# All 24 half matrices of the first four experts get homes of their own, LayerNorm parameters are spread by TensorE, identity products fill TensorE's waits

## The reference

```
for l in range(DEPTH):                                   # DEPTH = 2
    mix = hybrid_mixer(x, w_in[l], w_ret_o[l], w_dsa_o[l], w_out[l])
    h = layer_norm(DEEPNORM_ALPHA * x + mix, ln1_g[l], ln1_b[l])
    ffn = hierarchical_moe(h, ...)     # each row: 2 of 32 SwiGLU experts
    x = layer_norm(DEEPNORM_ALPHA * h + ffn, ln2_g[l], ln2_b[l])

expert_block: (silu(xb @ w_gate[e]) * (xb @ w_up[e])) @ w_down[e]
```

## Time and profile before

| what | us |
|---|---|
| median of 3 runs (1638.46 to 1639.27) | 1638.96 |
| the profiled execution | 1637.93 |
| its span in the trace | 1636.1 |

### The profile page before, as it was taken

One profiled execution on the slowest core, in us unless ns is written; L12 is line 12 of the kernel. 1 busy time (PEld: TensorE's weight loads), 2 busy tenths in 40 slices (PEclk: granted clock), 3 DMA queues, 4 the chain that ended last, 5 costly groups with the idle time before them and its releaser, 6 DMA issues. The chain is left out here.

```text
span 1636.1 us, 20903 instructions
## 1 busy us (share of the span) xinstructions
PE 1278.9 (78%) x8502; PEld 864.8 (53%) x8502; DVE 621.0 (38%) x1049; ACT 379.9 (23%) x423; POOL 0.2 (0%) x4
## 2 busy tenths in 40 slices
PE   8999999998546656656699999999985566556646
PEld 7998789984212212212188987899842122112211
DVE  5788576654100100100277875865631001000102
ACT  4334634322000000000143346343220000000000
POOL 0000000000000000000000000000000000000000
PEclk9999999999878877878889999999997688778778
DMA  8455346689999999999945453374999999999996
GB/s 297 157 195 198 121 155 228 215 355 419 427 424 428 429 429 424 428 428 429 404 169 181 155 205 133 126 278 167 411 418 428 427 427 428 427 427 427 428 426 248
DMA packets 96501, 528.72 MB, mean 323 GB/s; under 512 B 5425, under 2 KB 9905, under 8 KB 66737
## 3 DMA queue, kind: packets, MB, share of 16 engines
q1 hardware_dynamic: 94560, 523.10, 79.3%
q10 hardware_dynamic: 1872, 4.66, 0.8%
HBM read 526.69 MB, written 1.05 MB: 323 GB/s over the span
## 5 line engine op out<-in xcount | busy, mean ns | idle before, releaser
L912 PE MATMUL psum<-ring,aqT 128*32 128x512 f32 x1536 | 284.5, 715 | 131.0 <-PEq L900 131.0
L1510 DVE TENSOR_TENSOR w_low<-ring,w_high 128x2048 fp32r<-128x2048 f32 (+2 forms) x108 | 239.8, 2260 | 69.1 <-DVEq L1509 67.8
L1111 ACT ACTIVATE w_high<-ring 128x2048 fp32r<-128x2048 f32 (+2 forms) x108 | 198.5, 1887 | 193.8 <-ACTq L1108 179.5
L912 PE MATMUL psum<-spare,aqT 128*32 128x512 f32 x256 | 136.5, 724 | 116.9 <-PEq L963 116.9
L912 PEld LDWEIGHTS psum<-ring,aqT 128*32 128x32 f32 x1536 | 73.3, 129 | 234.9 <-issue 234.9
L1728 DVE TENSOR_TENSOR qk<-psum,qk 128x512 f32<-128x512 f32 x16 | 11.1, 692 | 488.1 <-DVEq L1727 488.1
L912 PE MATMUL psum<-rv,tmp 128*32 128x512 f32 x240 | 122.8, 702 | 66.0 <-PEq L988 66.0
L662 PE MATMUL psum<-x_high,w_high 128*128 128x256 f32 x512 | 146.8, 287 | 0.0
L662 PE MATMUL psum<-x_high,w_low 128*128 128x256 f32 x512 | 143.3, 280 | 0.0
L662 PE MATMUL psum<-x_low,w_high 128*128 128x256 f32 x512 | 143.2, 280 | 0.0
L912 PEld LDWEIGHTS psum<-spare,aqT 128*32 128x32 f32 x256 | 30.3, 130 | 211.0 <-issue 211.0
(11 more groups left out here) (235 smaller groups left out, 2217.3 us busy)
## 6 DMA issues: line engine op xcount, KB each, us to landing
ring<-in_w_gate_dram SPq DMA_DIRECT2D x56, 2048.0 KB, 33.6
ring<-in_w_in_dram SPq DMA_DIRECT2D x34, 2048.0 KB, 7.9
ring<-in_w_up_dram SPq DMA_DIRECT2D x28, 2048.0 KB, 22.3
spare<-in_w_up_dram SPq DMA_DIRECT2D x14, 2048.0 KB, 14.3
rv<-in_w_down_dram SPq DMA_DIRECT2D x12, 2048.0 KB, 31.2
rg<-in_w_down_dram SPq DMA_DIRECT2D x12, 2048.0 KB, 35.6
x_xT<-in_w_down_dram SPq DMA_DIRECT2D x12, 2048.0 KB, 40.0
ring<-in_w_down_dram SPq DMA_DIRECT2D x12, 2048.0 KB, 29.3
```

The lines of the kernel that those rows point to most:

```text
L912: mm = nc.tensor.matmul(bank[s, :], lhs[:, c, s], w[:, k, n * NB:(n + 1) * NB], start=(c == 0), stop=(c == chunks - 1))
L1111: nc.scalar.activation(half_tile(high, to, w, b), half_tile(ring, i % RAW, w, b), ACT.Copy).then_inc(high_ready, 1)
L1510: V.tensor_tensor(half_tile(low, i % RAW, w, b), half_tile(ring, i % RAW, w, b), half_tile(high, of, w, b).bitcast(f32), ALU.subtract).the ...
```

## The change

1. The buffer `stage` (free when retention's decayed scores are used up) and the second half of `qk` (`qk1`) become homes. Unit 1 goes to `stage` and unit 23 to `table`, both behind the load of ret00; unit 22 takes the place of unit 0 at out1; unit 0 goes to `qk1`, third in `FIRST`. No unit waits for `half_used[0]` any more. SP waits for a new semaphore `stage_free` ahead of unit 1.
2. `ln_params` is gone. `load_params` on ACT's queue loads the four parameter rows as 2 x 512 elements each into eight partitions of `tmp`. `spread` multiplies a column of the identity, repeated 128 times, with these rows, so that one row comes out on all partitions of a PSUM bank. `spread_first` does so for ln1 (four products) after the first quad's up; DVE reads it there. `spread_second` does so for ln2 ahead of the last quad, in two steps of two products, and ACT copies each into `lnp`.
3. `stay_warm` writes products of the identity with itself to a PSUM bank that nobody reads: 11 in layer 0 ahead of the first sweep, 24 in layer 1 ahead of the wait for the closing norm and 5 behind `XT0`.

```diff
-EARLY = [(10, "spare0", "rg0"), (11, "spare1", "rg0"), (16, "rv1", "dsa0"), (1, "table", "ret00"),
-         (18, "rg0", "out1"), (0, "qk0", "out1")]
+EARLY = [(10, "spare0", "rg0"), (11, "spare1", "rg0"), (16, "rv1", "dsa0"),
+         (23, "table", "ret00"), (1, "stage", "ret00"), (18, "rg0", "out1"), (22, "qk0", "out1")]
...
+                            if home == "stage":
+                                sp.wait_ge(stage_free, 1).then_inc(stage_free, -1)
                             load_first(l * NE, u)
...
-                             half0=half_used[0],
...
                 e = l * NE + QUAD
+                used(0)
                 load(e, 0, 0)
                 used(1)
...
+            def stay_warm(times):
+
+                for _ in range(times):
+                    nc.tensor.matmul(bank_y[0][:, 0:P], ident, ident, start=True, stop=True)
...
                     turn_row("XT1", x, 1)
+                    stay_warm(11)
                     pe.wait_ge(x_high_ready[l], 1)
...
+                    stay_warm(24)
                     pe.wait_ge(x_ready, 1).then_inc(x_ready, -1)
                     turn_row("XT0", x, 0)
+                    stay_warm(5)
                     pe.wait_ge(x_high_ready[l], 1)
...
+            def spread(row, bank):
+
+                return nc.tensor.matmul(bank, ident[0:8, row:row + 1].broadcast_to((8, P)),
+                                        param_rows, start=True, stop=True)
+
+            def spread_first():
+
+                pe.wait_ge(lnp_in, 64).then_inc(lnp_in, -64)
+                pe.wait_ge(job_free[JOB["HT1"] % GROUPS], 1)
+                pe.wait_ge(job_free[JOB["RL"] % GROUPS], 1)
+                for row in range(4):
+                    mm = spread(row, psum[:, row, :])
+                mm.then_inc(params_full_v, 1)
+
+            def spread_second():
+
+                pe.wait_ge(tg_copied, 1)
+                for c in range(2):
+                    spread(4 + 2 * c, bank_g)
+                    spread(5 + 2 * c, bank_u).then_inc(params_full_a, 1)
+                    pe.wait_ge(params_copied, 1).then_inc(params_copied, -1)
...
+                if last:
+                    spread_second()
                 arrived(0, 0, landed)
...
+                if first:
+                    spread_first()
                 if not last:
                     pe.wait_ge(picked, 2).then_inc(picked, -2)
                     gather()
...
-            def ln_params(g, b, l):
-                for n, v in enumerate((g, b)):
-                    act.dma_start(lnp[:, n, :], v[bass.ds(l, 1)].broadcast_to((P, D))
+            def load_params(l):
+                for n, v in enumerate((ln1_g, ln1_b, ln2_g, ln2_b)):
+                    act.dma_start(param_rows[2 * n:2 * n + 2, :],
+                                  v[bass.ds(l, 1)].rearrange("a (r n) -> (a r) n", r=2)
                                   ).then_inc(lnp_in, 16)
+
+            def copy_params():
+                both = psum[:, 4:6, :].rearrange("p b c -> p (b c)")
+                for c in range(2):
+                    act.wait_ge(params_full_a, 1).then_inc(params_full_a, -1)
+                    nc.scalar.activation(lnp[:, c, :], both, ACT.Copy).then_inc(params_copied, 1)
...
-                act.wait_ge(lnp_free, 4).then_inc(lnp_free, -4)
-                ln_params(ln2_g, ln2_b, l)
...
+                copy_params()
                 experts(last=True)
```

## The result

| what | before | after |
|---|---|---|
| median of 4 runs each | 1638.71 us | 1623.69 us |
| lowest and highest | 1636.21, 1639.27 | 1621.71, 1626.75 |
| the profiled execution | 1637.93 us | 1623.04 us |
| its span | 1636.1 us | 1621.3 us |

The ratio is 0.9912 with an interval of 0.9900 to 0.9924: 14.4 us less, from 12.5 to 16.4 (the two medians are 15.0 apart). The median of the changed kernel is 1.9 us under the 1625.6 that were predicted.

What follows compares the result with a forecast made beforehand. Full DMA engines bound the expert stages, PE's chain the mixers and layer turns. Transfers −9.8, layer 1's identity products −3.2 and layer 0's −0.4 make −13.4 us: 1638.96 to 1625.6 us, range 1623.0 to 1631.0.

Steps and rivals of the forecast that it cites:

- What bounds the kernel: Expert stage: DMA engines full, so time is bytes and PE work is free within waits; mixer and layer turns: PE's chain.
- The transfers: Expert stage: one unit and ln2's parameter loads leave the full DMA stretch, −4.9 us per layer, −9.8 us for both.
- One unit: Expert stage: seven units go out early instead of six, so one 1024 KB unit leaves the full stretch, −2.46 us per layer.
- ln2's rows: After the first quad: two 512 KB parameter DMAs go; bounds nothing to 2.46 us, upper end taken, −2.46 us per layer.
- The hole behind units 22 and 23: First quad's release: whole matrices go out at once with one more unit ahead, so the queue stays full; no gain counted.
- more than the sum: Rival: the queue runs more evenly where thin (417 against 427 GB/s over 89 us), −2 us more, 1623.5 us; chance 0.12.
- SP's wait: At ret00 SP waits for `stage_free`, given 4.8 us early: cost nothing. As a slower rival, 1656 us; slower had chance 0.03.
- PE's spreading: First quad: four products, 3.7 us between up and gather; second quad's gate about a microsecond late, taken up by waits, cost nothing.
- The second spreading: Ahead of the last quad: 6.5 us, 10 us at the lower clock, in a wait of 10.78 us; cost nothing.
- Identity products: Fill PE's waits to keep the higher clock: −3.2 us at the turn to layer 1, −0.4 us at layer 0's start.
- the clock does not hold: Rival: identity products gain nothing, 1629.2 us, or start low in layer 1 and outlast the wait, 1634; chance 0.15.
- The rival for layer 0: Layer 0's start: transposes don't count as busy, so the 11 products start at the low clock; loses up to 2 us.

Runs made afterwards that it cites:

- e9: Changed kernel with each spreading product taken over all 128 rows of the parameter buffer in place of 8; 1623.77 us, ratio 0.9913.
- e7: Kernel before with the 40 identity products alone, none of the transfers changed; 1635.43 us, ratio 0.9988.
- e11: Kernel before with the 40 identity products and seven more ahead of the last wait of each layer; 1633.92 us, ratio 0.9977.
- e4: Changed kernel with unit 23 issued last of the first quad's units, into the same, long free home; 1627.65 us, ratio 0.9938.
- e3: Changed kernel with ln2's gamma and beta loaded by two 512 KB DMAs after the first quad, in place of the second spreading; 1628.86 us, ratio 0.9942.
- e10: Changed kernel with 48 identity products in place of 24 ahead of the wait for layer 0's closing norm; 1628.01 us, ratio 0.9935.
- e1: Changed kernel without all 40 identity products; 1628.03 us, ratio 0.9942.
- e2: Changed kernel with the homes and order of the first quad's units as before, spreading and identity products kept; 1629.36 us, ratio 0.9948.
- e5: Changed kernel run again with no edit, beside the kernel before; 1625.13 us, ratio 0.9928.
- e6: Changed kernel with seven more identity products ahead of the last wait of each layer; 1622.80 us, ratio 0.9917.
- e8: Changed kernel with 12 identity products in place of 24 ahead of the wait for layer 0's closing norm; 1624.02 us, ratio 0.9916.

## Why the prediction came out right, point by point

**What bounds the kernel.** Right. The sixteen expert stages with the new transfers agree within 0.9 us, whatever PE does in them; e9 gives PE back 3.4 us in the first quad, and no stage follows.

**The transfers.** Predicted −4.9 us a layer, measured −5.19 and −6.03 in the first pair of traces, and −5.8 between the means of the kernels with new and old transfers (459.59 against 465.36, the latter of before, e7 and e11, whose six stages last 464.76 to 466.74). The mechanism was right, the size was short by 0.9 us a layer. By term:
- One unit: 2.46 predicted, 2.15 measured (e4).
- ln2's rows: 2.46 predicted, the upper of the two bounds; 3.30 measured (e3), some 3.0 without the slow start of that run. The reason given (no gaps at a share of 1.01) holds.
- The hole behind units 22 and 23: the step failed here. "The engines therefore have more to do at that moment than before" was the right reading, and no value was put on it. It is worth 0.7 to 1.1 us a layer on average, with much scatter, and it is what the rival "more than the sum" spoke of: that put 2 us for both layers on a more even queue, and its place is these four microseconds, not the 89 us, whose rate only rose from 417 to 419.

The three terms undone one at a time come to 6.6, more than the 5.8 of all together; 0.8 us is left over, about what the ±0.3 of each allows.

**SP's wait.** Costs nothing, as predicted; `stage` goes out 0.11 us behind the end of `table`'s issue.

**PE's spreading.** "Four such, 3.7 us" was wrong, and so was the price of what follows. The row it rested on (`start_sums`) has 128 rows on the array, these have 8, and the clock falls under them: 6.6 us in layer 0 (404.53 against 397.93), of which 3.2 remain when the clock stays up (e9: 401.13) and 3.4 are the clock. So the gate of the second quad started at 415.16, 3.9 us late, where the prediction had about one, and its wait was used up. That it costs nothing held: the homes came free 6.6 us late, and the queue had some 20 us in hand. The second spreading took 5.6 us (1553.81 to 1559.37) against an estimate of 6.5, and left a gate wait of 5.57 us. In 7 of the 16 with 8 rows (eight kernels) the clock fell in it, as the prediction had allowed; it then took 7.0 us and the wait left was 2.6 to 3.1, still enough. With 128 rows it fell in none of four.

**Identity products.** Layer 1: −3.2 us predicted, −3.24 measured, and 14.34 to 14.40 in all twelve traces against 17.58 and 17.63 without. The rival "the clock does not hold" falls for this place in all twelve traces; its dearest form, products that outlast the wait, costs 5.0 us (e10) and doesn't occur. Layer 0: −0.4 predicted, −0.36 in the pair of traces, by the step that was named, DVE's remainder:

```profile
21.02 3.96 DVE L1552 TENSOR_TENSOR w_low<-ring,w_high 128x1792 fp32r<-128x1792 f32 x2 [4.82 <-DVEq L1551]
...
23.19 0.44 PE L594 MATMUL psum<-w_high,x_high 128*128 128x448 f32 x1 [0.49 <-PEq L574]
```

Against an execution like e1's the gain is 1.5 us. So the term was read from an execution of before in which the clock rose early, and on average it is probably larger; one trace of each kind can't say by how much.

The rival for layer 0, that the clock is still low when the 11 products start, came out in part. In ten of the fourteen traces, the changed kernel's among them, all 16 transposes of the first turn took 421 ns or more; in four (before, e2, e7, e11) the last ones took 272, with nothing but transposes before them. In the changed kernel the first records of the identity products still took 421 ns and the others 275, and by the first sweeps the clock was up, as it was in all twelve traces with the products. Without them (e1) it was not. In five traces (e3, e4, e5, e6, e9) the slower products pushed the first sweeps back to 11.26 to 11.92 us, from 10.72 to 11.12 in the others, but tile ka, which waits for DVE, stayed between 23.16 and 23.52. So the prediction generalised from the one trace it had, and the loss of up to 2 us that it feared didn't come. Part 4 of the Trainium skill's page "TensorE: Matmul & The Clock Gate" says that transposes don't count as PE-busy in the same way as other products; the four traces, with float32 transposes, disagree, the ten others can't tell. Part 1 of the same page of the Trainium skill says that the chip's look at PE is not in step with the kernel. That fits: the same code has ends of 11.2 and 12.7 us, and runs of one kernel lie 5 us apart. The prediction put too little on that. It took the 0.8 us between the three runs of before for the whole scatter, and later runs of that same kernel, on two chips, lie from 1634.83 to 1641.87.

**The number.** −13.4 predicted. The four comparisons of the changed kernel, or its e9 twin, with the kernel before give −14.9 (profiles), −14.4, −11.8 and −14.2 (ratios 0.9912, 0.9928, 0.9913): the forecast lies among them. The first median fell beside the 1623.5 of "more than the sum", 1.9 us under the forecast. The stages account for 1.4 of that in the pair of traces (11.2 gained, 9.8 predicted). A long end costs 1.5 us and moves a run by as much as that, so how much of the place of this one median is luck can't be told. Of the signs that were named, the clock was 1.00 from the last down products to tile ka in the changed kernel's trace, but not in those with a long end (e4: 0.60).

## What to carry to other kernels

Where the DMA engines are full, count bytes in the full stretch, and look in it for the few microseconds in which the rate dips: a load that waits for a release with too little queued before it costs a term of its own. PE's idle stretches on the path can be filled with products that nobody reads, but only up to the wait (each microsecond over it is paid), and not necessarily all of it (in one trace 12 held the clock as well as 24). Compare parts of a trace before medians when a clock changes from run to run: the part said 3.3 us where two medians said 1.2.

## What was not expected of the hardware

- Products with 8 of the 128 rows mostly did not keep the clock up, without any gap on PE: in the changed kernel 1.00 at 392 us and 0.50 over 396 to 400, and a fall in or behind them in 15 of 18 first quads. The same products with 128 rows kept it at 1.00 in four of four.
- A gap of 2.86 us left the clock at 1.00 (e8), one of 2.98 us was followed by 0.60 over the next 4 us (e4), and gaps between 2.55 and 2.72 us went both ways. The two lengths of the end, 1.5 us apart, go with this: with seven products in the wait all six ends were short.
- One profiled execution can miss 3 us of it. The trace of before had an early rise at its start and two short ends, and e7's trace had two long ones.
